# Four products of the first output tile, moved from the head of one stage to the tail of the stage before

## The reference, cut to what matters

```
def merge_branches(p_gate, y_hy, y_att, w_hy_o, w_mla_o, w_out):
    g = jax.nn.sigmoid(p_gate)
    return (g[..., :D_MODEL] * (y_hy @ w_hy_o) + g[..., D_MODEL:] * (y_att @ w_mla_o)) @ w_out

hx = hx + g1x * merge_branches(px[..., MLA_END:], hy_x, att_x, w_hy_o[l], w_mla_o[l], w_out[l])
hx = hx + g2x * hier_moe(modulate(hx, norm2_g[l], sh2x, sc2x), *moe_w)
```

## Time and profile before

| | us |
|---|---|
| median of three runs | 2640.35 |
| the profiled execution, its own time | 2635.22 |
| its span (first to last instruction) | 2633.4 |
| TensorE matmuls busy | 2422.3 (92% of the span) |
| VectorE / ScalarE / GpSimd busy | 1073.3 / 621.5 / 691.3 |
| products with `w_out`, all of both layers, TensorE busy | 144.6 |

### The profile page before, as it was taken

The page is one execution under the profiler, slowest core; times in us unless marked ns, Lnnn a source line. Parts: engine busy times, 40 slices in busy tenths (PEclk is TensorE's granted clock), DMA queues, the critical chain, the costliest instruction groups (busy, mean ns, idle before and its releaser), DMA issues. The chain is left out here.

```text
span 2633.4 us, 35470 instructions
## 1 busy us (share of the span) xinstructions
PE 2422.3 (92%) x13020; PEld 1519.3 (58%) x13020; DVE 1073.3 (41%) x2144; ACT 621.5 (24%) x1374; POOL 691.3 (26%) x644
## 2 busy tenths in 40 slices
PE   7999988999999999998888899999999999988887
PEld 3455675555555565555554468645787665555553
DVE  5764487444212663111111175944422732222222
ACT  4441122442110232221111142234211311111111
POOL 0003132565221012222221222246431022222221
PEclk9999999999999999999999999999999999999999
DMA  9982020021113539999999913012226599999996
GB/s 365 372 343 92 28 95 19 14 55 25 48 48 94 233 137 391 395 398 400 402 392 385 360 41 116 33 32 55 49 73 208 233 361 395 392 408 404 403 402 242
DMA packets 192142, 588.40 MB, mean 223 GB/s; under 512 B 48464, under 2 KB 110203, under 8 KB 135708
## 3 DMA queue, kind: packets, MB, share of 16 engines
q1 hardware_dynamic: 167525, 551.99, 55.5%
q0 software_dynamic: 22400, 29.42, 3.4%
q10 hardware_dynamic: 2103, 5.51, 0.5%
HBM read 581.44 MB, written 51.51 MB: 240 GB/s over the span
## 5 line engine op out<-in xcount | busy, mean ns | idle before, releaser
L2661 PE MATMUL ps<-w,moe_xt 128*64 128x256 f32 x2816 | 341.2, 397 | 61.3 <-DMA w<-in_w_up_e 59.0
L2801 POOL DMA_INDIRECT rows_out<-moe_rows_out,table x128 | 117.9, 921 | 738.5 <-DVE moe_rows_out L2866 375.1
L2661 PEld LDWEIGHTS ps<-w,moe_xt 128*64 128x64 f32 x2816 | 221.3, 142 | 150.8 <-issue 67.6
L2916 DVE TENSOR_TENSOR moe_gated<-ps,moe_gated 64x256 f32<-64x256 f32 x128 | 54.5, 426 | 501.0 <-ACT moe_gated L2885 500.9
L2885 ACT ACTIVATE moe_gated<-ps 64x256 f32<-64x256 f32 x128 | 48.2, 376 | 666.9 <-PE ps L2661 666.9
L2661 PE MATMUL ps<-early_w,moe_xt 128*64 128x256 f32 x1280 | 153.4, 394 | 28.3 <-DMA early_w<-in_w_up_e 28.3
L1706 POOL TENSOR_SCALAR attn_p<-attn_p,attn_rs 128x768 f32<-128x768 f32 (+1 forms) x80 | 155.4, 1951 | 81.2 <-DVE attn_rs L1880 80.7
L2669 PE MATMUL ps<-w,moe_ht 128*64 128x512 f32 x704 | 170.4, 604 | 2.3 <-issue 2.3
L2178 PE MATMUL ps<-w_out,mix 128*128 128x512 f32 x320 | 144.6, 602 | 7.0 <-PEq L150 7.0
L2902 DVE TENSOR_TENSOR moe_rows_out<-ps,moe_row_gate 64x512 f32<-64x512 f32 x128 | 88.1, 688 | 138.3 <-PE ps L2669 136.2
L2661 PEld LDWEIGHTS ps<-early_w,moe_xt 128*64 128x64 f32 x1280 | 101.8, 141 | 65.9 <-issue 31.7
(11 more groups left out here) (435 smaller groups left out, 4271.8 us busy)
## 6 DMA issues: line engine op xcount, KB each, us to landing
w<-in_w_gate_e SPq DMA_DIRECT2D x88, 1024.0 KB, 25.9
w<-in_w_up_e SPq DMA_DIRECT2D x88, 1024.0 KB, 29.5
w<-in_w_down_e SPq DMA_DIRECT2D x88, 1024.0 KB, 29.3
prep_w<-in_w_ada SPq DMA_DIRECT2D x24, 2048.0 KB, 16.0
early_w<-in_w_gate_e SPq DMA_DIRECT2D x40, 1024.0 KB, 25.7
early_w<-in_w_up_e SPq DMA_DIRECT2D x40, 1024.0 KB, 29.5
early_w<-in_w_down_e SPq DMA_DIRECT2D x40, 1024.0 KB, 29.7
w_merge<-in_w_in SPq DMA_DIRECT2D x32, 512.0 KB, 5.4
```

Of the source, the lines that this page charges most:

```text
L2661: last = nc.tensor.matmul(ps[k * SLOTS:(k + 1) * SLOTS, 0:DE], xt[:, c], wgu[:, k, c], start=c == 0, stop=c == KC - 1)
L2801: nc.gpsimd.indirect_dma_start(out=dram["y"], out_offset=bass.IndirectOffsetOnAxis(ap=m.table[0:SLOTS, j:j + 1], axis=0), in_=y[:, j % 2], ...
L2916: nc.vector.tensor_tensor(h[:, b % 2], m.ps[SLOTS:2 * SLOTS, b % 2, 0:DE], sg[SLOTS:2 * SLOTS, b % 2], ALU.mult).then_inc(s["h_done"], 1)
```

## The change

At the end of TensorE's part of the merge stage it waits for the first half of `w_out`, for seven finished chunks of `m.mix`, and for bank 0 (X) to have been read for the last time. Then it issues the first four chunks of half 0 of tile 0 into bank 0, opening the sum there. In the out stage the loop leaves these four out for j = 0 and goes on with chunks 4 to 7, which close the sum. The matmul loop becomes a function of its own, with the same instructions. It is done in both layers.

```
-def merge_stage(nc, m, l, a, streams, early, token_sums, then):
+def merge_stage(nc, m, l, a, streams, early, token_sums, out_early, then):
...
+            w_out, w_out_in = out_early
+            pe.wait_ge(w_out_in[0], 16)
+            pe.wait_ge(s["mix_done"], KC - 1)
+            pe.wait_ge(s["c11_done"], KC)
+            out_product(nc, m, w_out, X, 0, 0, range(KC // 2))
...
+def out_product(nc, m, w, bank, tile, half, chunks):
+
+    for c in chunks:
+        last = nc.tensor.matmul(m.ps[:, bank], m.mix[:, tile, c], w[:, half, c], start=c == 0, stop=c == KC - 1)
+    return last
...
-                tile = work[j][1]
-                for c in chunks:
-                    last = nc.tensor.matmul(m.ps[:, 2 * (j % 2) + half], m.mix[:, tile, c], w[:, half, c],
-                                            start=c == 0, stop=c == KC - 1)
+                last = out_product(nc, m, w, 2 * (j % 2) + half, work[j][1], half, chunks)
...
             for j in range(NT):
-                product(j, 0, range(KC // 2))
                 if j >= 1:
+                    product(j, 0, range(KC // 2))
                     turn(j - 1, 0)
                     turn(j - 1, 1)
                 product(j, 0, range(KC // 2, KC))
```

More of the change, by code:

```diff
@@ L2597, in mixers @@
         out_early = late.enter_context(nc.sbuf_tensor(f"w_out{l}", [P, 2, KC, 4 * P], F32, side="right")), signals("w_out_in", 2)
-        merge_stage(nc, m, l, a, streams, merge_early, token_sums, lambda sp: out_loads(sp, l, a["w_out"], out_early))
+        merge_stage(nc, m, l, a, streams, merge_early, token_sums, out_early, lambda sp: out_loads(sp, l, a["w_out"], out_early))
     return out_early
```

## The result

| | us |
|---|---|
| predicted | 2632.5 (2626 to 2640) |
| measured, median of five runs | 2624.75 (2620.05 to 2626.22) |
| the kernel before beside it, median of five | 2637.18 (2635.67 to 2643.16) |
| ratio to before | 0.9948, 95% interval 0.9935 to 0.996 |
| profiled execution after / its span | 2626.22 / 2624.4 (before 2635.22 / 2633.4) |

It was right that the change helps; its size was wrong. The chance given to faster by over 0.3% was 0.42, and that is what happened.

The account below looks back on a forecast made before the run. TensorE waits at the borders for VectorE and GpSimd, sets the out stage's pace, and waits for weight transfers in the expert stage. Gains of 5.1 and 2.6 us, 7.8 in sum, off 2640.35 gave 2632.5 us, range 2626 to 2640.

Parts of the forecast that it names:

- Borders: Merge to out stage: layer 0's border unmoved, 5.1 us gained; layer 1's 0.8 us later, 2.6 us gained.
- The waits, contention, the loads at the head: Merge stage's tail and out stage's head: three added waits, engines running beside moved records, and loads all cost nothing.
- some 5 before: Layer 0's first transposes in the out stage: cover of some 5 us before the change, 4 us after.
- What would be late next: Out stage's head: router's loads, gate rows and VectorE's additions were checked; none becomes the bound.
- The experts: Expert stages: bound by the weights' stream, whose start shifts with the out stage's end, so the gains pass on.
- rival 3: Expert stages: weight transfers hide layer 0's 5.1 us, giving 2637.7, or both gains, giving 2640.35; chance 0.14.
- Rival 5: Layer 1's experts: gathers fall behind more weights, making the kernel slower, 2648.5 us; chance 0.04.
- rival 4: First expert's product: its 3.0 us at slow clock go too, gain 10.8 us, 2629.6; chance 0.10.
- the term for slow spells: Out stage's head: time lost at 1.2 GHz, 1.69 us in layer 0 and none in layer 1, goes.
- rival 2: Layer 0's out stage head: slow spell typically absent or stays after the change; gain 6.1 us, 2634.2; chance 0.29.
- The base: Whole kernel: the gain was taken off the median of three runs, 2640.35 us.
- theory X: Whole kernel, from the follow-ups: gain of 10 to 12 us, its part beyond the borders from stages far from them.

Follow-up runs that it names:

- e7: Changed kernel with seven chunks moved instead of four: 2632.18 us, ratio 0.9987 to the kernel before.
- the first trace: Profile of the unchanged kernel before on which the prediction rests: profiled execution 2635.22 us, span 2633.4 us.
- e12: Changed kernel with 4 instead of 16 filling products at the very end of the out stage: 2627.81 us, ratio 0.9962 to the kernel before.
- e4: The move made in layer 1 alone, layer 0 as in the kernel before: 2632.18 us, ratio 0.9987 to the kernel before.

## Why the prediction was wrong in size

*Borders.* Right in each term. Layer 0: border unmoved (4.03 us after the last branch product, before and after), 5.1 us forecast at the head, 5.1 measured in six traces; out stage shorter by 4.9 to 5.2 us in five of them, 3.3 in the first. Layer 1: border 0.8 us later as forecast, 3.4 off the out stage, 2.6 net.

*The waits, contention, the loads at the head.* Nothing was lost, as forecast for four chunks. The cover of the first transposes was 4.4 us (VectorE done at 861.99, the transposes at 866.42) where 4 were forecast. The "some 5 before" was misread: before, the transposes began at 874.18 and the cover was 9.2 us. What would be late next was named wrongly: it is the next rows and ScalarE's copy, and of their cover nothing was left (e7).

*The experts.* The gains passed through both expert stages; rival 3 is out. In layer 0 the stage's length changed by +0.4, -0.6 and -0.6 us in the three traces of the changed kernel against the first trace. Over all traces it was 572.2 us in the mean of the four with layer 0's border as before, and 571.9 in the five with four chunks moved there and the filling products left as they were. Rival 5, a slower kernel, is out too.

*A slow spell elsewhere* (rival 4) did go, and it is easy to take for the missing part, as 10.8 us were forecast for it. The first expert's product in layer 0, 6.65 us in the earlier trace rows, took 5.07 to 6.65 in all four traces with layer 0's border as before. It took 3.67 in eight of the nine that fill this border in part or whole; the ninth is e12 (5.32), where other filling was taken out. In the changed kernel:

```profile
972.86 3.67 PE L2671 MATMUL ps<-w,moe_xt 128*64 128x256 f32 x32 [0.78 <-ACT moe_xt L2882]
```

But these spells cost 2.2 us in the mean of the four traces, and the means above differ by 0.3 +- 0.6. SyncE's first load comes 1.8 to 2.0 us after TensorE's first expert product begins, whether that product is slow or not, in every trace but e12's (978.77 and 980.75 before, 972.86 and 974.66 after). So the start of the weights' stream doesn't hang on it, and the spell was hidden for the most part: rival 4 comes near in the number and not by its mechanism.

*The step that failed* is in the sum, in two terms. The first is the term for slow spells, taken as 1.69 us in layer 0 and nothing in layer 1. Layer 0's was fixed, not chance, so rival 2 was wrong: 15.50 us in four traces of four. Layer 1's was mis-sized: it costs 0 and 1.4 us in the two traces of the kernel before, and 1.9 in the mean of all four traces with that border. With 0.7 to 1.9 us for it the sum becomes 8.5 to 9.7 us. The Trainium skill (TensorE: Matmul & The Clock Gate, Part 1) says that the number of slow matmuls after idleness varies between runs of one kernel. At layer 1's border the traces agree, with 0, 1.4, 3.0 and 3.0 us; at layer 0's they don't. The prediction had weighed this against layer 0's term only.

*The base* is the second term, and the larger. The median of before was 2640.35 with three runs and 2637.18 with five, so 3.2 of the 7.75 us between forecast and result aren't the change's. The prediction's own row said so: the profiled execution was 5.1 us below that median, and the difference was kept. From 2637.18 the forecast would have been 2629.4, still 4.6 us above the result.

*What stays open.* By the means the gain is 11.3 +- 0.8 us, and 8.5 to 9.7 are accounted for. Nor do the parts add up neatly: layer 1 alone gave 2.7 to 3.0 us, where 2.65 plus the spells make 3.3 to 4.5. The stages that the change doesn't touch (all but the merge and out stages) add up to 2032.5, 2031.4 and 2030.6 us in the three traces of the changed kernel, and to 2032.7 to 2036.1 in the other ten, with 2035.6 and 2032.8 for the kernel before and 2034.1 for e12, which has both moves too. In the means of three traces and two, the changed kernel is 7.9 us shorter in the touched stages and 2.7 in the others. That is theory X's second half, and why it should be so was not shown. A part of it is layer 1's expert stage. Against the first trace it was 0.6, 1.8 and 0.7 us shorter in the three traces of the changed kernel, 1.1 and 2.4 longer in those of layer 1 alone, 3.2 and 2.9 longer in those of layer 0 alone. Its first expert's product took 3.67 us in four traces of thirteen and 1.4 to 2.9 more in the other nine, whose stages are 2.2 us longer in the mean. It doesn't settle single traces: the first of the changed kernel has such a spell and a short stage, e4 has none and a long one.

## What to carry to other kernels

Where one engine waits at a border for others, independent work of the next stage moved into the wait is worth its own time, plus any slow clock that the idle stretch causes; count the second from several executions, as one trace may be the one without it, and look whether a spell that went was on the path at all. Stop soon after the border begins to move: here a border 0.8 us later still paid, while with borders 2.3 and 3.4 us later TensorE gained 0.3 us more at most up to the constants, and the loads issued behind the border were late. And take the base from the executions that you have rows of, when a median of three runs lies far from them.

## What the runs showed of the hardware

An idle stretch of TensorE of 4.03 us before a stage was followed by 1.7 us lost at 1.2 GHz in each of four traces; one of 2.96 us by 0, 1.4, 3.0 and 3.0 us lost in four; one of 2.31 us by 1.7 in one; one of 1.24 us by none in one; stretches of 0.3 and 0.6 us by none in 16 heads. Computing eight records twice in each layer to fill the first two stretches made the kernel 2.6 +- 0.8 us faster. The first expert's product, some 127 us behind the stretch of 4.03 us, took 5.07 to 6.65 us in all four traces with it and 3.67 in eight of the nine where the stretch was shortened to 2.31 us or less.
